# Four attention heads on one core: rotary scores in two passes, rotary projection by pairs of heads, values of all heads at once, head loop written out

## What is computed

```python
q = (rms_norm(c_q, q_norm[i]) @ w_uq[i]).reshape(B, S, MLA_HEADS, QK_HEAD_DIM)
kv = (rms_norm(c_kv, kv_norm[i]) @ w_ukv[i]).reshape(B, S, MLA_HEADS, QK_NOPE_DIM + V_HEAD_DIM)
q_nope, q_pe = q[..., :QK_NOPE_DIM], q[..., QK_NOPE_DIM:]        # 128 and 64 wide
k_nope, v = kv[..., :QK_NOPE_DIM], kv[..., QK_NOPE_DIM:]         # 128 and 128 wide
q_pe = apply_rope(q_pe, cos[:, :, None], sin[:, :, None])
k_pe = apply_rope(k_rope, cos, sin)[:, :, None]                  # one for all heads
q = jnp.concatenate([q_nope, q_pe], axis=-1)
k = jnp.concatenate([k_nope, jnp.broadcast_to(k_pe, ...)], axis=-1)
mla_out = causal_mla(q, k, v)                                    # softmax(q k^T) v, causal
# apply_rope: [t1*cos - t2*sin, t2*cos + t1*sin] of the halves t1, t2
# beside it: hm = mlstm_chunkwise(mq, mk, m_v, gates), chunks of rows with a carried state
```

## Time and profile before

| what | value |
|---|---|
| median of 3 runs | 1882.0 us (1880.86 to 1884.81) |
| the profiled execution's own time | 1885.15 us |
| its span | 1883.3 us |
| PE busy | 1836.3 us, 98% |
| DVE, ACT, POOL busy | 1367.2, 642.0, 1080.0 us |
| the attention: from the end of the input projection to the output projection | about 251.6 to 439.0 us |

### The profile page before, as it was taken

One profiled execution on the slowest core, in us unless ns is written; L12 is line 12 of the kernel. 1 busy time (PEld: TensorE's weight loads), 2 busy tenths in 40 slices (PEclk: granted clock), 3 DMA queues, 4 the chain that ended last, 5 costly groups with the idle time before them and its releaser, 6 DMA issues.

```text
span 1883.3 us, 23545 instructions
## 1 busy us (share of the span) xinstructions
PE 1836.3 (98%) x8908; PEld 1541.9 (82%) x8908; DVE 1367.2 (73%) x1526; ACT 642.0 (34%) x1132; POOL 1080.0 (57%) x780
## 2 busy tenths in 40 slices
PE   7999999999999999999999999999999999989998
PEld 6888989987887888888878888887788888878786
DVE  6777135566677676576679989667878875799896
ACT  4432147763332111111133433515433343333214
POOL 3343322243038998888878786632565465568565
PEclk9999999999999999999999999999999999999999
DMA  5111110013231233231456641113233232941232
GB/s 164 46 46 45 54 21 21 20 45 112 101 112 45 79 129 124 79 117 62 162 202 219 239 138 52 45 45 113 91 110 112 108 121 85 355 158 68 90 112 89
DMA packets 121700, 194.73 MB, mean 103 GB/s; under 512 B 30065, under 2 KB 85873, under 8 KB 118530
## 3 DMA queue, kind: packets, MB, share of 16 engines
q1 hardware_dynamic: 121568, 193.34, 30.2%
q10 hardware_dynamic: 34, 0.07, 0.0%
HBM read 144.56 MB, written 48.82 MB: 103 GB/s over the span
## 4 chain that ended last, share of the span: by engine, by line
PE 85%; DVE 6%; POOL 3%; issue 3%; ACT 2%; DMA 0%; DVEq 0%; SPq 0%; ACTq 0%; POOLq 0%
PE ps L1108 72%; PE ps L1274 2%; PE ps L1296 2%; PE ps L1378 1%; PE ps L1379 1%; PE ps L1380 1%; POOL ring_lo L986 1%; PE ps L1286 1%; POOL ring_hi L985 1%; DVE y L2902 1%; DVE y L2895 1%; DVE xs_lo L2735 0%; ACT xs_hi L2051 0%; POOL d_w_lo L1060 0%; DVE m_lo L2776 0%
## 5 line engine op out<-in xcount | busy, mean ns | idle before, releaser
L1108 PE MATMUL ps<-f_hi,ring_hi 128*128 128x512 f32 x384 | 149.7, 390 | 1.3 <-POOL ring_lo L986 1.3
L1108 PE MATMUL ps<-f_lo,ring_hi 128*128 128x512 f32 x384 | 149.4, 389 | 0.0
L1108 PE MATMUL ps<-f_hi,ring_lo 128*128 128x512 f32 x384 | 149.4, 389 | 0.0
L896 POOL TENSOR_TENSOR w_lo<-stage,w_hi 128x1024 fp32r<-128x1024 f32 x48 | 125.7, 2619 | 4.0
L1108 PE MATMUL ps<-d_w_hi,d_hid_hi 128*128 128x512 f32 x312 | 121.5, 390 | 1.5 <-DVE hid L2601 1.1
L986 POOL TENSOR_TENSOR ring_lo<-w_sum,ring_hi 128x512 fp32r<-128x512 f32 x80 | 117.9, 1474 | 6.7
L1108 PE MATMUL ps<-d_w_hi,d_hid_lo 128*128 128x512 f32 x312 | 121.4, 389 | 0.0
L1108 PE MATMUL ps<-d_w_lo,d_hid_hi 128*128 128x512 f32 x312 | 121.4, 389 | 0.0
L1049 POOL TENSOR_TENSOR ring_lo<-w_sum,ring_hi 128x512 fp32r<-128x512 f32 x60 | 95.3, 1597 | 43.6 <-ACT ring_hi L2028 43.6
L893 POOL TENSOR_TENSOR cols<-ones 128x1 f32<-128x1 f32 x48 | 25.6, 533 | 162.3 <-PE ps L1108 145.7
L1928 ACT ACTIVATE f_copy<-ps 128x512 f32<-128x512 f32 x60 | 35.3, 596 | 225.2 <-PE ps L1108 206.3
(11 more groups left out here) (450 smaller groups left out, 5764.8 us busy)
## 6 DMA issues: line engine op xcount, KB each, us to landing
d_raw<-hid_rows SPq DMA_DIRECT2D x37, 512.0 KB, 4.3
stage<-in_w_up SPq DMA_DIRECT2D x22, 512.0 KB, 4.5
wd_raw<-in_w_down SPq DMA_DIRECT2D x22, 512.0 KB, 5.0
raw_w<-in_w_gate SPq DMA_DIRECT2D x20, 512.0 KB, 5.0
stage<-in_w_in SPq DMA_DIRECT2D x18, 512.0 KB, 3.6
stage<-in_pool_w_in SPq DMA_DIRECT2D x16, 512.0 KB, 5.1
raw_w<-in_pool_w_in SPq DMA_DIRECT2D x16, 512.0 KB, 4.9
m_rows<-u_row SPq DMA_DIRECT2D x16, 512.0 KB, 2.6
```

The costliest lines, as they stand in the source:

```text
L896: g.tensor_tensor(lo, stage[:, h, :], hi.bitcast(F32), ALU.subtract).then_inc(parted[h], 1)
L1108: last = mm(out_ap, l, r, start=(start and j == 0), stop=(stop and j == n - 1), skip_group_check=onto)
```

## The change

1. **Rotary queries summed.** The rotary projection is made for two heads at once: one product gives 128 rows, the 64 of head A and the 64 of head B, and a second one the same with halves exchanged. DVE multiplies the first by `rot`, the second by `rot_swapped`, and adds them. The result is rotated queries of both heads, 64 rows each.
2. **Two score passes.** ACT rounds the head's 64 rows into one half of `q_stack`, and DVE writes their low part into the other half. One full pass of `q_stack` by `k_pe_hi` gives high by high and low by high, a second one over the head's 64 rows alone gives high by `k_pe_lo`. Three passes were there before.
3. **Values of all heads at once**, before the first head: 8 blocks of 3 matmuls of 512 columns, `all_values`, and 16 copies on ACT, `take_values`. The projections between the heads have no values.
4. **Recurrence.** Heads 0 to 2 read their rows straight from `m_qk`; only head 3 is copied (`last_head_rows`). The scale of its keys goes to the copy of the chunk rows and to `s_t`.
5. **Moves.** `head_rows` of the last head, and `gate_head`, stand in the first step of the next head, and the loop over heads is written out on every engine. Odd and even heads have different orders: even heads take new rotary projections in front, odd ones find theirs made.

```diff
-                    passes = [(q, k) for q, k in ((q_n_hi, k_n_hi), (q_n_hi, k_n_lo), (q_n_lo, k_n_hi),
-                                                  (q_pe_hi, k_pe_hi), (q_pe_hi, k_pe_lo), (q_pe_lo, k_pe_hi))]
+                    turned = PAIR_B if h % 2 else PAIR_A
+                    passes = ((q_n_hi[:, blk], k_n_hi[:, cs]), (q_n_hi[:, blk], k_n_lo[:, cs]), (q_n_lo[:, blk], k_n_hi[:, cs]),
+                              (q_stack[:, blk], k_pe_hi[:, cs]), (q_stack[turned, blk], k_pe_lo[turned, cs]))
...
+            def all_values():
+                pe.wait_ge(heads_split, 1)
+                for t in range(TB):
+                    pe.wait_ge(in_taken, 36 + t + 1)
+                    ts = slice(t * P, (t + 1) * P)
+                    three(ps[:, (4 + t) % 8, :], [(c_kv_hi[:, ts], c_kv_lo[:, ts], wv_hi[:], wv_lo[:])]).then_inc(up_full, 1)
...
+            def up_rotary(h, n):
+                if h == 0 and n == 1:
+                    pe.wait_ge(up_taken, 8)
+                elif n == 1:
+                    pe.wait_ge(qp_ready, turned_at(h) + 1)
+                elif h:
                     pe.wait_ge(st_ready, 8 * h)
+                for e in range(2):
+                    latent_rows(ps[:, turned_bank(h, n, e), :], wqr_hi, wqr_lo, slice(P * e, P * e + P), n).then_inc(up_full, 1)
...
             def head_steps(h):
-                pe.wait_ge(up_taken, 6 * h + 6)
+                pe.wait_ge(up_taken, taken_at(h + 1))
                 pe.wait_ge(up_split, 4 * h + 4)
-                pe.wait_ge(qp_ready, h + 1)
-                pe.wait_ge(mk_nat, 2 * h + 2)
-                pe.wait_ge(mqkv_ready, 3 * h + 3)
+                pe.wait_ge(qp_ready, turned_at(h) + 6 + 2 * (h % 2))
                 chunk_scores(h, 0)
                 scores(h, 0)
+                if h:
+                    head_rows(h - 1, (2, 3))
+                pe.wait_ge(mk_nat, 2 * h + 2)
...
-            pe.wait_ge(in_taken, 44)
             pe.wait_ge(latent_split, 1)
-            up_queries(0, first=True)
-            up_rotary(0, first=True)
-            up_keys_values(0, first=True)
+            all_values()
+            up_queries(0)
+            up_rotary(0, 0)
+            up_rotary(0, 1)
+            up_keys(0)
             chunk_rows(0)
             pe.wait_ge(kpe_split, 1)
-            with pe.Fori(0, HEADS - 1, 1) as h:
+            for h in range(HEADS - 1):
                 head_steps(h)
                 up_queries(h + 1)
                 probs_transposed(h, TB - 1)
-                up_rotary(h + 1)
-                values(h, TB - 1)
-                up_keys_values(h + 1)
+                if h % 2:
+                    up_rotary(h + 1, 0)
+                    values(h, TB - 1)
+                    up_rotary(h + 1, 1)
+                    up_keys(h + 1)
+                else:
+                    up_keys(h + 1)
+                    values(h, TB - 1)
                 chunk_rows(h + 1)
-                pe.wait_ge(up_taken, 6 * h + 12)
-                head_rows(h, (2, 3))
+                pe.wait_ge(pt_taken, 8 * h + 8)
...
+            def take_turned(h, n):
+                act.wait_ge(qp_ready, turned_at(h) + 2 + 2 * n)
+                if h:
+                    act.wait_ge(s_full, 8 * h)
+                rows = PAIR_B if h % 2 else PAIR_A
+                f(q_stack[rows, half(n)], q_pe[rows, half(n)], ACT.Copy).then_inc(up_taken, 1)
...
-            head_copies(0, first=True)
-            copy_values(0, first=True)
+            take_values()
             take_queries(0)
-            take_keys_values(0)
+            copy_values(0)
+            take_turned(0, 0)
+            take_turned(0, 1)
+            take_keys(0)
             take_chunk_rows(0)
...
                 head_steps(h)
-                head_copies(h + 1)
                 take_queries(h + 1)
+                if h % 2 == 0:
+                    take_turned(h + 1, 0)
                 take_probs_t(h, TB - 1)
                 row_squares(h, TB - 1).then_inc(hsq_ready, 1)
-                take_out(h, TB - 1)
-                copy_values(h + 1)
-                finish_head(h)
-                take_keys_values(h + 1)
-                take_chunk_rows(h + 1)
+                if h % 2 == 0:
+                    take_turned(h + 1, 1)
+                    take_keys(h + 1)
+                    take_out(h, TB - 1)
+                    finish_head(h)
+                else:
+                    take_out(h, TB - 1)
+                    finish_head(h)
+                    take_turned(h + 1, 0)
+                    if h + 1 == HEADS - 2:
+                        last_head_rows()
+                    take_turned(h + 1, 1)
+                    take_keys(h + 1)
+                take_chunk_rows(h + 1)
+                copy_values(h + 1)
...
-            def rotary_queries(h):
+            def turn_queries(h, n):
+                if h or n:
+                    dve.wait_ge(qp_ready, turned_at(h) + 2 * n)
+                dve.wait_ge(up_full, up_at(h) + 4 + 2 * n)
+                own.mark(v.scalar_tensor_tensor(q_pe[:, half(n)], ps[:, turned_bank(h, n, 0), :], QK_SCALE, rot[:, half(n)],
+                                                ALU.mult, ALU.mult))
+                v.scalar_tensor_tensor(q_turned[:], ps[:, turned_bank(h, n, 1), :], QK_SCALE, rot_swapped[:, half(n)],
+                                       ALU.mult, ALU.mult).then_inc(qp_ready, 1)
+                own.wait(dve)
+                dve.wait_ge(qp_ready, turned_at(h) + 1 + 2 * n)
+                v.tensor_tensor(q_pe[:, half(n)], q_pe[:, half(n)], q_turned[:], ALU.add).then_inc(qp_ready, 1)
+
+            def turned_low(h, n):
+                here, there = (PAIR_B, PAIR_A) if h % 2 else (PAIR_A, PAIR_B)
+                dve.wait_ge(up_taken, taken_at(h) + 3 + n)
+                v.tensor_tensor(q_stack[there, half(n)], q_pe[here, half(n)], q_stack[here, half(n)].bitcast(F32),
+                                ALU.subtract).then_inc(qp_ready, 1)
...
             split_queries(0)
-            rotary_queries(0)
+            dve.wait_ge(early_act, 5)
+            turn_queries(0, 0)
+            turn_queries(0, 1)
+            turned_low(0, 0)
+            turned_low(0, 1)
             split_keys(0)
...
-                rotary_queries(h + 1)
-                norm_head(h)
+                if h % 2:
+                    head_sums(h)
+                    turn_queries(h + 1, 0)
+                    norm_head(h)
+                    turn_queries(h + 1, 1)
+                    turned_low(h + 1, 0)
+                    turned_low(h + 1, 1)
+                else:
+                    turned_low(h + 1, 0)
+                    head_sums(h)
+                    turned_low(h + 1, 1)
                 split_keys(h + 1)
-                gate_head(h)
```

More of the change, by code:

```diff
@@ L1200, in pe_program @@
             in_tile(9, 1, 40, 0)
-            def latent_rows(o, c, n):
-                cs, ts = slice(c, c + P), slice(n * HALF, (n + 1) * HALF)
-                return three(o, [(wq_hi[:, k, cs], wq_lo[:, k, cs], c_q_hi[:, k, ts], c_q_lo[:, k, ts]) for k in range(2)])
-            def up_queries(h, first=False):
-                pe.wait_ge(heads_split, h + 1)
-                if not first:
+            def all_values():
[4 more added lines that the diff above has]
+                    three(ps[:, (4 + t) % 8, :], [(c_kv_hi[:, ts], c_kv_lo[:, ts], wv_hi[:], wv_lo[:])]).then_inc(up_full, 1)
@@ L1213, in up_queries, with latent_rows @@
+            def latent_rows(o, w_h, w_l, cs, n):
+                ts = slice(n * HALF, (n + 1) * HALF)
+                return three(o, [(w_h[:, k, cs], w_l[:, k, cs], c_q_hi[:, k, ts], c_q_lo[:, k, ts]) for k in range(2)])
+            def up_queries(h):
+                pe.wait_ge(heads_split, h + 2)
+                if h:
                     pe.wait_ge(probs_done, 8 * h)
                 for n in range(2):
-                    latent_rows(ps[:, n, :], 0, n).then_inc(up_full, 1)
-            def up_rotary(h, first=False):
-                if not first:
+                    if h == 0:
+                        pe.wait_ge(up_taken, 5 + n)
+                    latent_rows(ps[:, n, :], wqn_hi, wqn_lo, slice(0, NOPE), n).then_inc(up_full, 1)
@@ L1761, in act_program @@
             act.wait_ge(latent_ready, 1)
+            f(rot_swapped[PAIR_A, :], rot[PAIR_B, :], ACT.Copy)
+            f(rot_swapped[PAIR_B, :], rot[PAIR_A, :], ACT.Copy).then_inc(early_act, 1)
             for c in range(HEADS):
@@ new lines, in copy_values, with take_values @@
+            def copy_values(h):
+                if h:
+                    act.wait_ge(cn_full, 8 * h)
+                f(vo[:, :, 0:P], m_v[:, :, h * P:(h + 1) * P], ACT.Copy).then_inc(mqkv_ready, 1)
+            def take_values():
+                for t in range(TB):
+                    act.wait_ge(up_full, t + 1)
+                    b = (4 + t) % 8
+                    f(v_first[:, t, :], ps[:, b, 0:P], ACT.Copy)
```

(9 more changed lines are left out.)

203 lines of the change are left out of this document (103 added, 100 removed).

## The result

| kernel | median | kernel before, same chip | ratio, 95% interval |
|---|---|---|---|
| changed | 1898.2 us | 1881.8 us | 1.0083 (1.0071 to 1.0096) |

Forecast were 1879.6 us, with 1871 to 1892 as the range. The time lies above the range, and the direction was wrong as well: the change makes the kernel 0.8% slower. 1.0083 is 15.6 us. The profiled execution of the changed kernel is the shortest of its four, 1894.36 us; the others took 1897.9 to 1902.3.

A forecast was written before the change was run, and what follows sets the result against it. PE was taken as the bound, with 14.4 us removed but 11 to 12 eaten by waits. Start +6.4 - 0.8, odd heads 2 x -3.1, even +3.1, inside -4.8, with loop returns -2.4: 1882.0 to 1879.6 us, range 1871 to 1892.

The forecast's parts named there:

- What bounds the kernel: Whole kernel: PE, busy 98% of the span; time comes off only where its list shortens, and new waits lose it.
- Removed from PE, -14.4: PE's list: third rotary pass 8.5 us, values 5.1, start of projections 0.8 removed, if no wait took their place.
- Rival C: Score passes: 96 changes between 64-row and full-row matmuls cost time; 0.09 us each gives 1888.2, far end 1899; chance 0.27.
- The start of the first head: Projections before the first head: +6.4 us, with a new 2.5 us wait, then -0.8 in its first two blocks.
- Into odd heads, -3.1 each: First query matmul to second step's transposes, twice: 21.2 us becomes 18.1, with 3.0 of new waits.
- Into the even head, +3.1: Same stretch into head 2, with rotary work of two heads: 21.2 us becomes 24.3, including a 2.7 us wait.
- Inside the heads, -4.8: Rest of each head, from the removed rotary pass: three heads gain 1.3 us each, the last one 0.9.
- The sum: Whole kernel: all steps together -2.3 us, with three loop returns -2.4, from the median 1882.0 to 1879.6.
- D: Starts of heads 0 and 2: waits of 2.5 and 2.7 us also lower the clock, 1.1 to 1.6 each; 1882.2; chance 0.08.
- rival A: Whole kernel: the forecast itself, 1879.6 us, with waits eating 11 to 12 of the 14.4 us; chance 0.45.
- B: New waits on PE come to only half of those found: -8.4 us, 1873.6; chance 0.20.
- What the profile will show: Expected signs: last pass's starts 0.23 us apart or 0.3 and more; waits of 2.5, 2.7 and twice about 1 us.

The follow-up runs named there:

- e5: The changed kernel with the last score pass over all 128 rows and 30 matmuls of no use in PE's waits before the heads: 1882.4 us, 1.0005.
- e4: The kernel before without its sixth score pass (q_pe_lo by k_pe_hi), nothing else changed: 1876.7 us, 0.9968.
- e1: The changed kernel with the last score pass over all 128 rows instead of the head's 64: 1888.5 us, 1.0027.

## Why the prediction was wrong, step by step

**What bounds the kernel.** Right: PE's list and its waits made up the result. Only "time comes off where PE's list gets shorter" left out that a matmul's price depends on its neighbour's shape.

**Removed from PE, -14.4.** The count holds. The step that failed is the price of the 64-row pass, "I take that of the removed pass's neighbours, 0.229 for 512 columns". Measured are 0.10 us going in and 0.20 coming out at 512 columns, 0.30 a pair; by the same reading 0.27 at 384 columns (two starts in 0.63 instead of 0.36), 0.30 at 256 (0.52 instead of 0.22) and 0.24 at 128 (0.46 instead of 0.22). That is 20 x 0.30 + 12 x 0.27 + 12 x 0.30 + 4 x 0.24 = 13.8 us on PE, 0.14 a change, of which 8 to 10 reach the time, since the last head hides its share. Rival C had the mechanism and bounds around it (0.11 and 0.2), but I took 0.09 between two rows neither of which shows a change of shape, and gave it 0.27. The second of its two "nearest rows", the whole load unhidden, was nearer. That C's far end, 1899, lies beside the measured 1898.2 is luck: it stands for 19 us of shape changes, of which there are 8 to 10, and the clock makes up the rest. The Trainium skill (TensorEngine Tiling (Array Packing), Key Properties) says that a change of the tiling mode drains TensorE, and gives no size. The trace agrees as far as it shows a delay at each of the two changes, 0.10 and 0.20 us; it does not show what the array does in it.

**The start of the first head.** Forecast were 18.7 us from the input projection's end (251.6 to 270.3). Measured: 267.96 - 249.05 = 18.9. The wait forecast at 2.5 was 2.91, for the same tile, `k_n_lo`. Counted from the projection's end DVE's last addition ended at 16.0 us (forecast 16.0), ACT's rounding at 16.6 (16.6), the keys' copy at 17.6 (17.6), DVE's low parts at 18.7 (18.7). Right, link by link. The gain of 0.8 behind it was too large: the two first blocks have 0.11 + 2 x 0.229 = 0.57 less by the forecast's own prices, not 0.9, and in e5 the second transposes come 6.0 us later than before, not 5.6.

**Into odd heads, -3.1 each.** Forecast were 18.1 us from the first query matmul to the second transposes; the changed kernel took 320.40 - 302.05 = 18.35 into head 1, and e5, without shape changes, 18.2. Waits: forecast 1.2 for `k_n_lo` and 1.0 for `head_rows`, measured 1.09 and 1.0. Into head 3, though, it is 19.3 in e5, against 21.8 in before: 2.5 gained. That boundary already has DVE beside POOL; I had taken it to be like the first.

**Into the even head, +3.1.** Forecast 24.3, measured 23.95 in e5 (364.34 - 340.39); waits 0.3 and 2.91 against 0.4 and 2.7. Right.

**Inside the heads, -4.8.** From the second transposes to the next head's queries e5 took 1.3 to 1.35 us less than before in each of three heads: right. In the last head it took 0.3 us more where 0.9 less was forecast. I had seen that PE waits there and still let most of the pass count; e4 shows in the kernel before that none of it comes.

**The sum** without C and D was -2.4; e5 shows -0.4 in the section (187.2 against 187.6) and 1.0005 in the median. The 2 us lie in the last head (1.2), the last boundary (0.6) and the first head up to its second transposes (0.4), less 0.4 by which the even boundary came out shorter; the small rest is in the odd boundary, the heads and the loop returns, for which no row shows a gain (three of a tenth would also make 0.3 and not the 0.1 that the sum took). So rival A was right as far as it went, and B is out: the waits came in full.

**D** was under-sized. Forecast were 1.1 to 1.6 us for each of two waits, with a chance of 0.08. Measured: 3.0 us in a head whose start is at the slower level (33.4 against 30.4; 38.0 against 34.9), and behind the waits of about 1 us in front of odd heads it came twice in eight (34.2 against 33.2 in e1's head 1). The row I had scaled from, is the end of such a stretch and not its length. C and D are not alternatives but add up, which my chances, one case at a time, could not give: 1879.6 + 2 + 8.1 + 6.6 is 1896.3, against 1898.2 measured. Of the two, C's term was larger than D's, and it alone would have kept the kernel from getting faster.

**"What the profile will show"** named the right places: the starts of the last pass, 0.33 and 0.43, tell A from C in the changed kernel's own profile.

## What to carry to other kernels

Don't shrink one matmul of a row to 64 rows to save products; where the other operand can be made valid over all 128 rows (here `k_pe_lo` holds its rows twice, and the extra term only adds accuracy), the full-row form is the cheap one, and if it must be narrow, keep the narrow ones together. Count a new wait of PE at more than its length: add what the matmuls behind it lose at the slower clock, and before judging a change that shortens PE's list, fill the wait with other projections whose inputs are ready. And read each head or stage apart: what PE saves in a stage in which another engine is slowed is waited again.

## What the runs showed of the hardware that I had not expected

- A change between matmuls over 128 rows and over 64 costs 0.10 us going from 128 to 64 rows and 0.20 us back at 512 columns, and nearly the same at 256 (0.10 and 0.20) and 384 (0.09 and 0.19) and a little less at 128 columns (0.10 and 0.14). It does not grow with the columns.
- The same wait of 2.91 us in front of the first head left the granted clock at 1.00 in the changed kernel's profiled execution and was followed by 0.50 for five microseconds in e1's. Even two waits of about 1.1 us, with the transposes between them, were followed by windows of 0.78 and 0.88, in e1. That a median moves by 4 to 7 us on this alone is why single profiles of such kernels should not be compared by their spans.
- One multiplication on DVE, 128x256, took 0.35 us alone and 2.03 us beside POOL's splitting of weights; of 128x512 in the kernel before 0.49 and 1.53.
